# The last third of the last down projection in two halves of the tokens, with the output stored as whole rows

## The reference

```python
def rmsnorm(x, g):
    xf = x.astype(jnp.float32)
    y = xf * lax.rsqrt(jnp.mean(xf * xf, axis=-1, keepdims=True) + EPS)
    return (y * g.astype(jnp.float32)).astype(x.dtype)
...
def swiglu(h, w_gu, w_down):
    gu = h @ w_gu
    gate, up = jnp.split(gu, 2, axis=-1)
    return (jax.nn.silu(gate) * up) @ w_down
...
        x = x + 0.5 * swiglu(rmsnorm(x, ffn2_norm[l]), ffn2_w_gu[l], ffn2_w_down[l])
    return rmsnorm(x, final_norm)
```

## Time and profile before

| what | us |
|---|---|
| median of 3 runs | 1990.86 |
| their range | 1989.51 to 1991.07 |
| the profiled execution, its own time | 1988.77 |
| its span | 1987.0 |
| TensorE (PE) busy | 1940.8, 98% of the span |
| VectorE (DVE) busy | 992.2, 50% |
| ScalarE (ACT) busy | 751.4, 38% |
| GpSimd (POOL) busy | 246.1, 12% |

### The profile page before, as it was taken

One profiled execution on the slowest core, in us unless ns is written; L12 is line 12 of the kernel. 1 busy time (PEld: TensorE's weight loads), 2 busy tenths in 40 slices (PEclk: granted clock), 3 DMA queues, 4 the chain that ended last, 5 costly groups with the idle time before them and its releaser, 6 DMA issues.

```text
span 1987.0 us, 22614 instructions
## 1 busy us (share of the span) xinstructions
PE 1940.8 (98%) x9020; PEld 1576.9 (79%) x9020; DVE 992.2 (50%) x1488; ACT 751.4 (38%) x1110; POOL 246.1 (12%) x248
## 2 busy tenths in 40 slices
PE   8999999999999999999999999999899999999997
PEld 6777788878888887788888877877787788888886
DVE  6677534373333335643333466777654444333334
ACT  5344523453223224432322355555543343222233
POOL 5221001201011011110100131022010011011012
PEclk9999999999999999999999999999999999999998
DMA  5212223433333324233333222122231233333322
GB/s 163 85 54 64 64 85 95 117 96 96 100 100 97 96 80 122 85 96 97 100 100 96 85 85 64 54 64 64 75 96 54 85 96 96 96 97 98 101 80 58
DMA packets 343402, 175.71 MB, mean 88 GB/s; under 512 B 6305, under 2 KB 343298, under 8 KB 343298
## 3 DMA queue, kind: packets, MB, share of 16 engines
q1 hardware_dynamic: 343298, 174.27, 30.2%
HBM read 172.15 MB, written 2.10 MB: 88 GB/s over the span
## 4 chain that ended last, share of the span: by engine, by line
PE 91%; DVE 4%; ACT 2%; issue 1%; DMA 0%; SPq 0%; POOL 0%; DVEq 0%; ACTq 0%
PE ps L979 28%; PE ps L983 28%; PE ps L981 27%; PE ps L1039 1%; PE ps L1072 1%; PE ps L1019 1%; DVE WL L1403 1%; PE ps L1117 1%; PE ps L992 1%; PE ps L1135 1%; PE ps L1028 1%; PE ps L1009 1%; PE ps L1002 1%; DMA RAW<-in_w_in 0%; PE ps L1053 0%
## 5 line engine op out<-in xcount | busy, mean ns | idle before, releaser
L1403 DVE TENSOR_TENSOR WL<-RAW,WH 128x1024 fp32r<-128x1024 f32 (+2 forms) x336 | 400.8, 1195 | 690.3 <-ACT WH L1175 690.2
L979 PE MATMUL ps<-HH,WH 128*128 128x512 f32 x1728 | 689.2, 399 | 7.9 <-DVE TS L1436 7.9
L983 PE MATMUL ps<-HL,WH 128*128 128x512 f32 x1728 | 675.7, 391 | 1.9 <-DVE HL L1413 1.8
L981 PE MATMUL ps<-HH,WL 128*128 128x512 f32 x1728 | 674.9, 391 | 1.1 <-DVE WL L1403 1.1
L1175 ACT ACTIVATE WH<-RAW 128x1024 fp32r<-128x1024 f32 (+2 forms) x336 | 342.4, 1021 | 550.3 <-PE ps L983 542.4
L979 PEld LDWEIGHTS ps<-HH,WH 128*128 128x128 f32 x1728 | 325.4, 188 | 84.2 <-DVE TS L1436 9.1
L983 PEld LDWEIGHTS ps<-HL,WH 128*128 128x128 f32 x1728 | 325.4, 188 | 74.0 <-DVE HL L1413 5.3
L981 PEld LDWEIGHTS ps<-HH,WL 128*128 128x128 f32 x1728 | 325.6, 188 | 72.9 <-issue 5.3
L979 PE MATMUL ps<-GH,WH 128*128 128x512 f32 x720 | 281.7, 391 | 0.0
L983 PE MATMUL ps<-GL,WH 128*128 128x512 f32 x720 | 280.6, 390 | 0.0
L981 PE MATMUL ps<-GH,WL 128*128 128x512 f32 x720 | 280.2, 389 | 0.0
(11 more groups left out here) (181 smaller groups left out, 1448.2 us busy)
## 6 DMA issues: line engine op xcount, KB each, us to landing
RAW<-in_ffn_w_gu SPq DMA_DIRECT2D x88, 512.0 KB, 3.8
RAW<-in_w_in SPq DMA_DIRECT2D x68, 512.0 KB, 3.9
RAW<-in_ffn_w_down SPq DMA_DIRECT2D x32, 512.0 KB, 4.1
RAW<-in_w_gate SPq DMA_DIRECT2D x22, 512.0 KB, 3.8
RAW<-in_w_up SPq DMA_DIRECT2D x22, 512.0 KB, 3.8
RAW<-in_w_out SPq DMA_DIRECT2D x16, 512.0 KB, 4.2
RAW<-in_mem_w_kv SPq DMA_DIRECT2D x16, 512.0 KB, 3.9
RAW<-in_w_down SPq DMA_DIRECT2D x16, 512.0 KB, 4.2
```

Source lines behind the costliest of these rows:

```text
L979: e.matmul(bk, wh, xh, start=k == 0, stop=False)
L981: e.matmul(bk, wl, xh, start=False, stop=False)
L983: last = e.matmul(bk, wh, xl, start=False, stop=k == kt - 1)
L1403: e.tensor_tensor(m["WL"][:, s, 0:kt, :], m["RAW"][:, n % NRAW, 0:kt, :], m["WH"][:, s, 0:kt, :].bitcast(F32), ALU.subtract).then_inc(*sg. ...
```

## The change

The last third of the last down projection is taken out of `ffn`'s loop and made by `last_down`. It runs over two halves of the tokens (256 each) and within them over the eight tiles of features. Every half tile is a group of its own in `mtiles`, with its own entry in the list of weight slices, and the matmuls read columns `col0` to `col0 + 256`. The add, the gain, the square, the turn (two transposes) and its copy are made on 256 columns. The squares are summed on GpSimd from tile 1 to tile 6; tile 0's sum and tile 7's square are added by TensorE in the products of `finish`. After the copy a turned tile stands in `O[h]`, which has whole rows: 128 partitions x 2 token blocks x 1024 features, in the space of the buffers `L` and `PT` of the attention stages.

`finish(0)` stands behind the matmuls of the first tile of the second half and ahead of that tile's add; `finish(1)` at the end. Each scales its half in four blocks of 128 x 512 (two on VectorE, two on ScalarE; none on GpSimd) and stores each with one DMA of 256 KB, in runs of 2 KB.

```diff
-    def mtiles(self, specs, xs, banks, cols=T, ahead=True, before=None):
+    def mtiles(self, specs, xs, banks, cols=T, ahead=True, before=None, col0=0):
...
+            if n == 2 and gen == 5:
+                self.last_down(down, f0, nf, G)
+                return
...
-    def turn_out(self, c):
-        if c:
-            self.turn(("fg", c - 1), ("fg", c - 1), ("ot", c - 1), 4)
-        self.tiles.take(("fg", c))
-        self.step("final_gain", c)
-
-    def finish(self):
-        self.bank("fin")
-        self.step("finish")
-        self.turn(("fg", 7), ("fg", 7), ("ot", 7), 4)
-        self.step("finish_r")
-        for c in (0, 1, 2, 3, 5, 4, 6, 7):
-            self.step("store", c)
+    def last_down(self, down, f0, nf, G):
+        for h in range(2):
+            for mt in range(KD):
+                key = (h, mt)
+                b = self.bank(("lb", key))
+                mm, = self.mtiles([(down, f0, nf, mt * P)], ("G", G, 0), [b], 256, col0=256 * h)
+                if h and mt == 0:
+                    self.finish(0)
+                self.step("add_half", key, b, mm)
+                self.banks.give(b, ("xo", key))
+                if mt:
+                    self.turn_half((h, mt - 1))
+                self.tiles.take(("fg", key))
+                self.step("final_gain", key)
+                self.tiles.take(("so", key))
+                self.step("square_half", key)
+                if 0 < mt < KD - 1:
+                    self.step("square_half_add", key)
+                    self.tiles.give(("so", key), ("ao", key))
+        self.finish(1)
+
+    def finish(self, h):
+        self.bank(("fin", h))
+        self.step("finish", h)
+        self.tiles.give(("so", (h, 0)), ("fin", h))
+        self.tiles.give(("so", (h, KD - 1)), ("fin", h))
+        self.turn_half((h, KD - 1))
+        self.step("finish_r", h)
+        self.banks.give(("fin", h), ("fR", h))
+        for i in range(2):
+            for a in range(2):
+                self.step("store", h, i, a)
...
+    def turn_half(key, free):
+        h, mt = key
+        g.wait_ge(*sg.at("to", key))
+        wait_all(free)
+        e.activation(m["O"][h][:, :, mt * P:(mt + 1) * P], blocks(at.bank(("to", key))[:, 0:256], P),
+                     ACT.Copy).then_inc(*sg.inc("oc", key))
...
+    def store(h, i, a):
+        if i:
+            y = m["O"][h][:, i, a * T:(a + 1) * T]
+            g.wait_ge(*sg.at("fR", h))
+            g.wait_ge(*sg.at("oc", (h, KD - 1)))
+            e.activation(y, y, ACT.Copy, scale=m["ST"][:, h, i:i + 1]).then_inc(*sg.inc("oa", (h, a)))
...
+    def add_half(key, b, mm):
+        h, mt = key
+        x = X[:, mt, 256 * h:256 * h + 256]
+        g.wait_ge(*sg.at(*mm))
+        g.wait_ge(*sg.at("x", (6, mt, 1)))
+        e.scalar_tensor_tensor(x, at.bank(b)[:, 0:256], 0.5, x, ALU.mult, ALU.add).then_inc(*sg.inc("xo", key))
...
+    def store(h, i, a):
+        if i == 0:
+            y = m["O"][h][:, 0, a * T:(a + 1) * T]
+            g.wait_ge(*sg.at("fR", h))
+            g.wait_ge(*sg.at("oc", (h, KD - 1)))
+            e.tensor_scalar(y, y, m["ST"][:, h, 0:1], None, ALU.mult).then_inc(*sg.inc("ov", (h, a)))
...
+    def store(h, i, a):
+        c = slice(a * T, (a + 1) * T)
+        g.wait_ge(*sg.at("oa" if i else "ov", (h, a)))
+        e.dma_start(od[:, 2 * h + i, c], m["O"][h][:, i, c]).then_inc(*sg.inc(f"d_out{h}{i}{a}", 0, 16))
...
+        mem["O"] = [mem[n][:, :, 0:D] for n in ("LB", "PTB")]
```

More of the change, by code:

```diff
@@ L439, in evac @@
             self.banks.give(b, ("x", (gen, mt)) if last else ("x", (gen, mt, part)))
-            if last and nextcol is not None:
+            if last:
                 self.feed(gen, mt, nextcol, free)
-            elif last:
-                self.turn_out(mt)
-                self.square(("n", gen), mt, ("X", mt), T, ("x", (gen, mt)))
         return evac
@@ L1136, in memory_values, with finish @@
         o.then_inc(*sg.inc("mo", 2 * u + d))
[L1138 to L1144, removed]
+    def turn_half(key, free):
+        bk, t = at.bank(("to", key)), at.tile(("fg", key))
+        g.wait_ge(*sg.at("fg", key))
+        wait_all(at.bank_free(("to", key)))
+        for j in range(2):
+            i = e.transpose(bk[:, j * P:(j + 1) * P], t[:, j * P:(j + 1) * P], ident)
+        i.then_inc(*sg.inc("to", key))
+    def finish(h):
+        bk = at.bank(("fin", h))
+        g.wait_ge(*sg.at("ao", (h, KD - 2)))
+        wait_all(at.bank_free(("fin", h)))
+        for c in (0, KD - 1):
+            t = at.tile(("so", (h, c)))
+            if c:
+                g.wait_ge(*sg.at("so", (h, c)))
+            for j in range(2):
+                o = e.matmul(bk[:, j:j + 1], t[:, j * P:(j + 1) * P], m["onesD"][:, 0:1], start=c == j == 0, stop=c > 0,
+                             skip_group_check=True)
+        o.then_inc(*sg.inc("fin", h))
     todo = dict(gain0=gain0, gain1=gain1, turn_x=turn_x, memory_turn=memory_turn, mm=mm, sum_square=sum_square,
@@ L1316, in memory_probs, with final_gain, square_half, turn_half @@
         e.activation(m["PT"][u % 2][:, j * T:(j + 1) * T], at.bank(("mj", u, j)), ACT.Copy).then_inc(*sg.inc("mq", (u, j)))
[L1318 to L1319 removed]
+    def final_gain(key):
+        if key == (0, 0):
+            explog()
+    def square_half(key):
+        h, mt = key
+        g.wait_ge(*sg.at("xo", key))
+        wait_all(at.tile_free(("so", key)))
+        e.activation(at.tile(("so", key))[:, 0:256], X[:, mt, 256 * h:256 * h + 256], ACT.Square).then_inc(*sg.inc("so", key))
+    def turn_half(key, free):
+        h, mt = key
[3 more added lines that the diff above has]
+                     ACT.Copy).then_inc(*sg.inc("oc", key))
+    def finish(h):
+        r, bk = m["ST"][:, h, 0:2], at.bank(("fin", h))
         explog()
[L1321 to L1322 removed]
+        g.wait_ge(*sg.at("fin", h))
+        e.activation(r, bk[:, 0:2], ACT.Ln, bias=m["eps"][:, 0:1], scale=4.0).then_inc(*sg.inc("fr"))
         g.wait_ge(*sg.last("fr"))
[L1324 to L1336, removed]
+        e.activation(r, r, ACT.Exp, scale=-0.5).then_inc(*sg.inc("fr", h))
+    def store(h, i, a):
[4 more added lines that the diff above has]
+            e.activation(y, y, ACT.Copy, scale=m["ST"][:, h, i:i + 1]).then_inc(*sg.inc("oa", (h, a)))
     todo = dict(split=split, feed=feed, square=square, rstd=rstd, normed=normed, plain=plain, turn=turn, split_tile=split_tile,
@@ L1669, in finish_r @@
         g.wait_ge(*sg.last("fv"))
-        e.scalar_tensor_tensor(a, bk[:, 0:4], 1e-6, a, ALU.add, ALU.mult).then_inc(*sg.inc("fv"))
+        e.scalar_tensor_tensor(a, bk[:, 0:2], 1e-6, a, ALU.add, ALU.mult).then_inc(*sg.inc("fv"))
         g.wait_ge(*sg.last("fv"))
[L1672 to L1679, removed]
+        e.scalar_tensor_tensor(R, a, 3.0, R, ALU.subtract, ALU.mult, reverse0=True).then_inc(*sg.inc("fR", h))
@@ L1855, in sync_program @@
             todo[kind](*a)
-    for c in range(KD):
-        g.wait_ge(*sg.at(f"d_out{c}", c))
+    for h in range(2):
+        for i in range(2):
+            for a in range(2):
+                g.wait_ge(*sg.at(f"d_out{h}{i}{a}", 0))
 def program(nc, dram, out):
```

60 lines of the change are left out of this document (32 added, 28 removed).

## The result

The median of 16 runs is 1993.92 us (1991.73 to 1996.04), that of 16 runs of the kernel before 1990.49. The ratio is 1.0019, 95% interval 1.0012 to 1.0026: a rise of 3.4 to 3.8 us, just inside the 0.2% that I had called no measurable change, and the interval excludes no loss at all. The forecast was 1993.9.

What follows compares the result with a forecast made beforehand. TensorE was taken to bound the kernel (91% of the span), with a tail of 14.62 us after it. A stage 9.3 us longer and a tail 6.2 shorter gave +3.1, median 1993.9, range 1990.6 to 1997.0.

Steps and rivals of the forecast that it cites:

- The first half tile: Start of the last down projection's last third: still waits for the late gate tile, ends at 1940.78; 2.2 us lost.
- The matmuls: TensorE's half tiles: 18 matmuls on 256 columns at 0.1195 us each, 2.15 us a half tile, not 2.05.
- The relay: Steady half tiles: round, split, add, gain, hand-over make the turn ready after 2.88 us; two half tiles take 5.27.
- The first finish: Inside the second half's stream: half tiles 9 and 10 take 6.84 us, not 5.27; 1.6 us lost.
- The clock: Rival: after TensorE's stands the granted clock falls for one half tile; net +5.2 us, 1996.1; chance 0.05.
- The tail: After the last product, to the end of the span: 14.62 us becomes 8.4, so -6.2 (5.9 to 6.8).
- a sign of being wrong: Final stores: the prediction is wrong if the last megabyte takes less than 2.8 us or more than 3.7.
- The sum: Whole kernel: stage +9.3 us and tail -6.2 us give net +3.1 us (+1.8 to +4.3).
- rival 1: Half tiles: product-to-turn chain longer than costed; over 0.2% slower from 2.71 us each, 1997.2 at 2.9; chance 0.18.
- Rival 3: Half tiles: the turn is not late, they take 2.39 us, net -0.6, 1990.3; chance 0.12.
- Rival 4: DMA engines: doubled slice loads and the first 1 MB of stores delay a slice, 1 us at most, 1995; chance 0.03.

Runs made afterwards that it cites:

- experiment 4: Changed kernel, with VectorE splitting the next weight slice after the add and gain of a half tile, not before: 1990.97 us, 1.0000 of the kernel before.
- experiment 7: Changed kernel, with every turn one half tile later on TensorE: 1988.67 us, 0.9996 of the kernel before.
- experiment 6: Changed kernel, with the first finish's factor and scaled passes moved behind add, gain and square of half tile 8: 1993.99 us, 1.0019 of the kernel before.
- experiment 2: Kernel before, with only whole-row copies, scaled blocks of 128 x 512 and 2 KB store runs, nothing halved: 1988.54 us, 0.9991 of the kernel before.
- experiment 1: Changed kernel, with stores back in runs of 512 bytes, same bytes and count of stores: 1994.77 us, 1.0024 of the kernel before.
- experiment 5: Changed kernel, with add and gain before split, first two half tiles grouped, first half's turns later, first finish later: 1986.28 us, 0.9980 of the kernel before.

## Why the prediction was right, step by step

**The first half tile.** Forecast to end 4.36 us after the stage begins (1936.42 to 1940.78); measured 4.36. It is half the work in the same time, a loss that no matmul count shows.

**The matmuls.** 0.1195 us forecast; 0.119 measured (1946.12 to 1948.03, 16 steps). The Trainium skill's page "TensorE: Matmul & The Clock Gate", section "Back-to-back issue gap", would have had 0.109; the trace goes with the row of the memory tiles.

**The relay.** Forecast 2.88 from the end of a half tile to its turn and 5.27 for two; the parts came as 0.88, 0.88, 0.45, 0.41 and two half tiles took 5.29. That this relay binds, and not TensorE's own work, is shown by two edits that shorten or defer it and do nothing else: both bring the period to 2.37 (experiments 4 and 7). I had forecast a wait of 0.5 before every other turn; the profile shows 0.2. It counts idle time from the modelled end of the last matmul, 0.28 after its start, though the next would have started 0.12 after it: from 1953.33 to the turn at 1953.82 are 0.49, so 0.37 is lost. The rest of the 0.55 lies around the turn between, which comes late too. The loss of time was right, its look in the trace not.

**The first finish.** Forecast 6.84 from the end of half tile 8 to the turn after half tile 10, measured 1964.07 to 1970.84, 6.77. I had said that one wait of some 1.5 us would be seen there, and it is 0.83: in the same time TensorE makes the narrow products of the finish (1964.07 to 1964.93), 0.86 us that my account of its work left out. They lengthen nothing, since the relay is the longer way. The price of moving the finish alone was as worked out in advance, nil (experiment 6).

**The clock.** I gave it 0.05 as a rival and it happened, in half of the six profiles that have the same stand. My reason against it failed: the idle time before the narrow products had been as long in the trace of before, without a fall. The same stand can be followed by a fall or not, and that very one, 1.93 us without, is 1.99 with a fall in experiment 2. The price was too high as well: I had 2.1 us for 18 matmuls, but at half clock they are 0.213 apart, not twice 0.12. With the order of the change it costs little: stages with it take 45.94 and 45.97, without it 45.21 and 45.32, so 0.7, because half tile 1, 1.4 us longer, runs into a turn that would have waited 0.6 anyway (0.58 in experiment 1). The forecast left it out, and its profile was 0.7 above the forecast stage for this alone.

**The tail.** 8.4 forecast, 8.0 measured. The factor was ready 0.2 us later than forecast (2.7 us after the last turn forecast, 2.9 measured, 1983.70 to 1986.61). The mis-sized term is the rate of the stores: I took a value between 284 and 371 GB/s and near the lower; it is 380. At that rate 1.05 MB take 2.76 us, just under the 2.8 that I had named as a sign of being wrong; the time came out right all the same. The Trainium skill's page "DMA: Bandwidth & Descriptors", section "Specifications", has line rate from 512 bytes on; in this kernel 2 KB runs move a third more bytes at the same busy share, and experiment 1 turns that off and on by the length of the runs alone.

**The sum.** Forecast 9.3 - 6.2 = +3.1; measured in the profile 10.0 - 6.6 = +3.4, of which 0.7 is the clock. Two small errors, +0.7 and -0.4, met. The median came within 0.1 us, nearer than the method can claim: that is luck, and the same kernel again had 1992.89, a ratio of 1.0013.

**Rivals.** The period stayed under 2.71, so rival 1 didn't come. Rival 3's period of 2.39 is what the orders of experiments 4 and 7 give, and its sum of -0.6 is close to experiment 7's -0.5 in the profile. Rival 4, the loads: no wait for a load or a split slice is among TensorE's waits of this stage.

## What to carry to other kernels

Cutting the last stage in halves shortens the tail, but everything that was hidden under a full tile must now hide under half of one. Write the relay from the end of a tile to the first thing the tensor engine needs of it as a sum, and compare it with the shorter tile: here 2.88 against 2.39, where it had been 3.3 against 4.6. What breaks it is mostly order: work that isn't needed for two tiles (the next slice's split) stood ahead of work that is needed at once (the add), and putting it behind took the loss of 0.2% away (experiment 4), and together with three more orders it became a gain of 0.2%. An operand that comes late for the first tile can be met with a group of tiles (a stand of 0.15 us for 1.46), provided that the group's other work isn't put ahead of its first result.

## What the runs showed of the hardware

Stores of 256 KB each moved 282 to 289 GB/s in runs of 512 bytes and about 380 in runs of 2 KB (369 to 391 in windows of 1 us), all 16 DMA engines being fully busy in both cases. Experiment 1 changes the length of the runs and neither the bytes nor the number of stores.

Three of six profiles with the same idle time of 1.46 us on TensorE, followed by 0.22 more, show the granted clock at 0.50 for about 3 us soon after, and three don't. This isn't a matter of the shorter matmuls or of this stage: in the part that nothing changes, all ten profiles have a stand of 2.6 us near 1370 with matmuls of 512 columns behind it, and seven have a fall there, three (before, experiments 1 and 5) none. One fall there cost 1.6 us, so two profiles of one program can differ by more than many a change is worth. The Trainium skill's page "TensorE: Matmul & The Clock Gate", section "What's actually happening", says that the monitor which sets the clock is not in step with the kernel, so that the moment of a change varies; the traces agree with it. What would be needed to be safe from it was not tried; the one kernel with half tiles and no stand in this stage (experiment 5) kept the full clock there in its one profile.
